# Two chained transformer blocks on one core: four norms computed by halves, the last norm by row tile, a row tile's entry to block two moved into the expert stream, a lent buffer slot returned seven experts later

## The reference, cut to what matters

```python
# first block
h = rmsnorm(x, norm_mix_g);  proj = h @ w_in      # cb cc cx q k v gc ga
merged = sigmoid(gc) * y_conv + sigmoid(ga) * y_attn
x = x + merged @ w_mix_out                        # site "mx"
m = rmsnorm(mem, norm_mem_g)                      # norm ("mem", 1)
x = x + cross_attention(rmsnorm(x, norm_cross_g), m, w_cq, w_ckv, w_co)   # site "co"
hf = rmsnorm(x, norm_ffn_g)                       # norm ("ffn", h)
# peer_ffn: per token 8 heads x 16 experts of 16384, each a row of peer_u and one of peer_v
act = gelu(einsum('td,thkd->thk', hf, peer_u[experts]))
x = x + einsum('thk,thkd->td', g * act, peer_v[experts])
x = rmsnorm(x, final_g)                           # the entry to block two, tag "fa"
# second block
z = rms_norm(x, mix_norm_g) @ w_in                # norm ("mix2", h)
x = x + y @ w_out                                 # site "ou"
x = x + memory_cross_attention(x, mem, ...)       # norm ("x", 2, h), site "xo"
x = x + conv_ffn(x, ...)                          # norm ("ffn2", h), "up", "down"
return rms_norm(x, final_norm_g)                  # tag "fb"
```

## Time and profile before

| | us |
|---|---|
| median of 3 runs | 2889.5 |
| lowest and highest | 2885.08, 2890.11 |
| the profiled execution, its own time | 2889.16 |
| its span, first to last instruction | 2887.4 |
| PE busy | 2419.1 (84%) |
| DVE busy | 1731.8 (60%) |
| ACT busy | 1131.4 (39%) |
| POOL busy | 665.6 (23%) |
| mean of the 16 DMA engines | 290 GB/s |

### The profile page before, as it was taken

The page is one execution under the profiler, slowest core; times in us unless marked ns, Lnnn a source line. Parts: engine busy times, 40 slices in busy tenths (PEclk is TensorE's granted clock), DMA queues, the critical chain, the costliest instruction groups (busy, mean ns, idle before and its releaser), DMA issues.

```text
span 2887.4 us, 31469 instructions
## 1 busy us (share of the span) xinstructions
PE 2419.1 (84%) x11066; PEld 1663.3 (58%) x11066; DVE 1731.8 (60%) x4201; ACT 1131.4 (39%) x2791; POOL 665.6 (23%) x569
## 2 busy tenths in 40 slices
PE   8999999869978658888958678677985799988998
PEld 7786666657744327536626434353864466655873
DVE  2101311498797788676999888787999426312430
ACT  2101301242533765354442578555555224412210
POOL 0000000122344343332233344444323101000110
PEclk9999999989989879999979578888997799999999
DMA  6555343589999999999899999999999653433443
GB/s 206 172 151 165 102 140 130 203 337 372 402 411 416 414 391 390 419 400 397 307 352 396 366 369 420 413 419 418 417 418 417 226 168 106 147 124 95 153 153 116
DMA packets 160973, 838.77 MB, mean 290 GB/s; under 512 B 17400, under 2 KB 21896, under 8 KB 95024
## 3 DMA queue, kind: packets, MB, share of 16 engines
q0 software_dynamic: 73728, 536.90, 45.8%
q1 hardware_dynamic: 82464, 287.75, 28.8%
q10 hardware_dynamic: 4624, 12.11, 1.1%
HBM read 828.27 MB, written 8.41 MB: 290 GB/s over the span
## 4 chain that ended last, share of the span: by engine, by line
PE 52%; DVE 19%; DMA 12%; ACT 12%; issue 4%; POOL 1%; ACTq 0%; DVEq 0%; SPq 0%
PE ps L914 24%; DMA BIG<-in_uv,BIG 11%; DVE BIG L1956 6%; PE ps L1158 5%; PE ps L934 5%; PE ps L935 5%; DVE X L1933 4%; PE ps L915 3%; PE ps L1185 2%; ACT L1451 2%; DVE BIG L1864 1%; DVE BIG L1861 1%; POOL BIG L2173 1%; PE ps L1128 1%; PE ps L1107 1%
## 5 line engine op out<-in xcount | busy, mean ns | idle before, releaser
L2173 POOL DMA_INDIRECT BIG<-in_uv,BIG x512 | 622.5, 1216 | 1617.5 <-DVE BIG L1910 562.3
L914 PE MATMUL ps<-BIG,RING 128*128 128x256 f32 x3472 | 814.1, 387 | 15.0 <-DMA RING<-in_w_cq 4.8
L914 PEld LDWEIGHTS ps<-BIG,RING 128*128 128x128 f32 x3472 | 667.9, 194 | 149.5 <-issue 26.4
L1956 DVE CUSTOM_DVE_ANT_0 BIG<-BIG 128x1024 f32<-128x1024 f32 x512 | 619.0, 1218 | 98.8 <-DMA BIG<-in_uv,BIG 95.9
L1933 DVE SCALAR_TENSOR_TENSOR X<-BIG,small,X 128x1024 f32<-128x1024 f32 x304 | 389.6, 1282 | 74.9 <-ACT small L1455 74.8
L1451 ACT ACTIVATE small<-small 128x1 f32<-128x1 f32 x512 | 102.3, 200 | 607.4 <-DVE small L1956 602.7
L914 PE MATMUL ps<-WK,RING 128*128 128x256 f32 x1232 | 292.7, 391 | 22.4 <-DVE BIG L1712 20.6
L914 PEld LDWEIGHTS ps<-WK,RING 128*128 128x128 f32 x1232 | 239.6, 196 | 63.1 <-DVE BIG L1712 27.2
L934 PE MATMUL ps<-RING,BIG 128*128 128x512 f32 (+1 forms) x448 | 225.1, 584 | 5.6 <-DVE BIG L1691 2.4
L935 PE MATMUL ps<-RING,BIG 128*128 128x512 f32 (+1 forms) x448 | 223.5, 580 | 0.0
L1284 ACT ACTIVATE BIG<-ps 128x256 f32<-128x256 f32 (+2 forms) x143 | 56.5, 396 | 381.6 <-PE ps L915 325.5
(11 more groups left out here) (258 smaller groups left out, 2867.9 us busy)
## 6 DMA issues: line engine op xcount, KB each, us to landing
RING<-in_w_up SPq DMA_DIRECT2D x88, 512.0 KB
RING<-in_w_down SPq DMA_DIRECT2D x66, 512.0 KB
RING<-in_w_pq SPq DMA_DIRECT2D x32, 512.0 KB
RING<-in_w_cc SPq DMA_DIRECT2D x16, 512.0 KB
RING<-in_w_cx SPq DMA_DIRECT2D x16, 512.0 KB
RING<-in_w_cb SPq DMA_DIRECT2D x16, 512.0 KB
RING<-in_w_cv SPq DMA_DIRECT2D x16, 512.0 KB
RING<-in_w_gc SPq DMA_DIRECT2D x16, 512.0 KB
```

Source lines behind the costliest of these rows:

```text
L914: e.matmul(ps[:, 0:256], W[:, j, :], src[:, j, 0:256], start=j == 0, stop=False)
L1956: e.tensor_tensor_reduce(out=u, in0=HF[:, t % 2, :], in1=u, scale=1.0, scalar=0.0, op0=ALU.mult, op1=ALU.add, accum_out=dots[:, k % 8:k % ...
L2173: e.indirect_dma_start(out=slot[i], out_offset=None, in_=I["uv"], in_offset=bass.IndirectOffsetOnAxis(ap=IDX[:, t, c:c + 1], axis=0)).then ...
```

## The change

Six things are changed.

1. **The memory's norm.** In `mixer_0` its squares, root and scaling stay in place, its eight transpose pairs now follow the projection cb.
2. **Four norms by halves**, those in `QUICK`: ("x", 1, 0) behind site mx, ("ffn", 0) behind co, ("x", 2, 1) behind ou, ("ffn2", 1) behind xo. The residual of columns 0 to 511 is ready one group of four chunks earlier than that of columns 512 to 1023. ACT squares the first half then (`quick_first`), runs a square root that only brings in its table, and DVE prepares the mean. After the second half: squares 512 wide, root with the first half's mean as its bias, reciprocal, and scaling in two pieces of 512 columns. A transpose waits for its own half only.
3. **Slot 7** is taken back seven experts after `gates` (3, 3) has been chosen (`back_at`), so expert 300 and not 293 is the first in it.
4. **The entry to block two by row tile** (`enter`). For row tile 2 it now stands at the end of `work`, while the experts of row tile 3 run: gain row, squares, a root that brings in the table, mean, root, scaling, for "fa" and then "mix2". `second(1)` does this for row tile 3 only. The gain row has an address of its own, in the work area and not in half 1's area.
5. **`last(0)`** stands behind the transposes of ("x", 2, 1), its gain row is loaded behind ou, and its store on SP's queue behind the chunks of site xo.
6. **The last down projection.** Chunks 0 to 15 feed all four q as before. Chunks 16 to 21 are held in the six ring slots together, then used for q 0 and 1, for q 2 and for q 3. Behind q 0 and 1 comes the output norm of row tile 2 (`tail_sq`, `tail_out`, `tail_store`), behind q 3 that of row tile 3, both in halves of 512 columns, with the table brought in ahead, and four stores of 128x512. The tuple that `late_down` yields is only written otherwise.

```diff
+QUICK = {("x", 1, 0): "mx", ("ffn", 0): "co", ("x", 2, 1): "ou", ("ffn2", 1): "xo"}
...
-        if i >= (8 if self.lent_from is None or (3, 3) in self.chosen else 7):
+        if self.back_at is None and (3, 3) in self.chosen:
+            self.back_at = k + 7
+        if i >= (8 if self.lent_from is None or (self.back_at is not None and k >= self.back_at) else 7):
...
     def norm_steps(self, key, lean):
+        if key in QUICK:
+            for kind in ("quick_sq", "quick_inv", "quick_out"):
+                yield 0, kind, key
+            return
...
-        yield from self.norm(("mem", 1), False)
+        yield from self.norm_steps(("mem", 1), False)
         yield from self.proj_T("cb", 0, 2, False)
+        for k in range(8):
+            yield 0, "trans", ("mem", 1), k, False
...
         yield from self.norm(("x", layer, h), lean)
+        if layer == 2 and h:
+            yield from self.last(0)
...
+        if h:
+            yield from self.enter(1, 0)
...
         if h:
-            yield from self.last(0)
+            yield 0, "final_in", "fb", 0
         yield from self.cross(2, h, lean)
+        if h:
+            yield 0, "store", 0
...
-            for f in range(22):
+            for f in range(16):
...
+            ring = {f: self.next_ring() for f in range(16, 22)}
+            for f in ring:
+                yield 0, "chunk", "down", f, ring[f]
+            for qs in ((0, 1), (2,), (3,)):
+                for f in ring:
+                    yield 0, "down", h, f, ring[f], qs
+                if qs[-1] % 2:
+                    for kind in ("tail_sq", "tail_out", "tail_store"):
+                        yield 0, kind, qs[-1] // 2
...
         yield from self.second(0, True)
         self.light = True
+        while "total2" not in self.reached:
+            yield "wait"
+        yield 0, "final_in", "fa", 1
+        yield from self.enter(0, 4.0)
...
+            def quick_sq(key):
+                site, src = QUICK[key], norm_of(key)["src"]
+                for i in range(2):
+                    w.wait_ge(*at["ev", site, key[-1], 1, i])
+                    own()
+                    e.activation(SQ[:, 512:1024], src[:, i, 512:1024], ACT.Square, accum_out=small[:, 502 + i:503 + i]).then_inc(
+                        act.sem, act("sqb", key, i))
+                    own()
+                    w.wait_ge(*at["nb", key])
+                    e.activation(small[:, 506 + i:507 + i], small[:, 502 + i:503 + i], ACT.Sqrt, bias=small[:, 504 + i:505 + i],
+                                 scale=1.0 / 1024).then_inc(act.sem, act("rt", key, i))
```

More of the change, by code:

```diff
@@ L1145, in conv_out, with down @@
                     pe.sem, pe("mm", "ct", h, c))
-            def down(h, f, k, tiles):
+            def down(h, f, k, qs):
                 W = RING[:, k % 6, :]
@@ L1150, in down @@
                 w.wait_ge(*at["upm", h, f])
-                qs = [2 * t + hh for t in tiles for hh in range(2)]
                 for q in qs:
@@ new lines, in enter_root, with enter_out @@
+            def enter_root(kind, i):
+                v = small[:, ENTER_AT[kind] + i:ENTER_AT[kind] + i + 1]
+                w.wait_ge(*at["erec", kind, i])
+                e.activation(v, v, ACT.Sqrt).then_inc(act.sem, act("ert", kind, i))
+            def enter_out(kind, i):
+                if kind == "mix2" and i == 0:
+                    own()
+                    w.wait_ge(*at["ev", "up", 0, 10, 3])
+                    e.activation(TMPz[:, 0, :], X[:, 2, :], ACT.Copy, scale=small[:, ENTER_AT[kind]:ENTER_AT[kind] + 1]).then_inc(
+                        act.sem, act("nrm", ("mix2", 1), 0))
@@ L1619, in norm_out, with quick_first, quick_inv @@
                     dve.sem, dve("nrm", key, 1))
+            def quick_first(key):
+                w.wait_ge(*at["sqa", key, 1])
+                e.tensor_scalar(small[:, 504:506], small[:, 500:502], 1.0 / 1024, 1e-6, ALU.mult, ALU.add).then_inc(
+                    dve.sem, dve("nb", key))
+            def quick_inv(key):
+                o = norm_of(key)["o"]
+                for i in range(2):
+                    w.wait_ge(*at["rt", key, i])
+                    e.reciprocal(small[:, o + i:o + i + 1], small[:, 506 + i:507 + i]).then_inc(dve.sem, dve("ri", key, i))
+                at["rstd", key] = (dve.sem, dve.n)
@@ new lines, in quick_out, with enter_inv @@
+            def quick_out(key):
+                n = norm_of(key)
+                own()
+                for j in range(2):
+                    e.tensor_scalar(n["tmp"][:, 1, 512 * j:512 * j + 512], n["src"][:, 1, 512 * j:512 * j + 512],
+                                    small[:, n["o"] + 1:n["o"] + 2], None, ALU.mult).then_inc(dve.sem, dve("nrm", key, 1, j))
+            def enter_inv(kind, i):
+                v = small[:, ENTER_AT[kind] + i:ENTER_AT[kind] + i + 1]
+                w.wait_ge(*at["esq", kind, i])
+                w.wait_ge(*at["ahead", kind, i])
+                e.tensor_scalar(v, v, 1.0 / 1024, 1e-6, ALU.mult, ALU.add).then_inc(dve.sem, dve("emean", kind, i))
+                own()
+                e.reciprocal(v, v).then_inc(dve.sem, dve("erec", kind, i))
@@ new lines, in tail_out @@
+            def tail_out(i):
+                w.wait_ge(*at["tsq", i, 0])
+                e.tensor_scalar(small[:, 518 + i:519 + i], small[:, 508 + 2 * i:509 + 2 * i], 1.0 / 1024, 1e-6, ALU.mult,
+                                ALU.add).then_inc(dve.sem, dve("tb", i))
+                w.wait_ge(*at["trt", i])
+                e.reciprocal(small[:, 520 + i:521 + i], small[:, 520 + i:521 + i]).then_inc(dve.sem, dve("trec", i))
+                own()
+                w.wait_ge(*at["fb", 1])
+                for hh in range(2):
+                    sl = slice(512 * hh, 512 * hh + 512)
+                    e.scalar_tensor_tensor(out=OUT[1][:, i, sl], in0=X[:, 2 + i, sl], scalar=small[:, 520 + i:521 + i],
+                                           in1=FG1["fb"][1][:, sl], op0=ALU.mult, op1=ALU.mult).then_inc(
+                        dve.sem, dve("fin", 1, i, hh))
@@ L2102, in y_scale, with down @@
                         e.tensor_scalar(Y[h][:, i, a:b], Y[h][:, i, a:b], small[:, o:o + 1], None, ALU.mult).then_inc(dve.sem, dve(*sig))
-            def down(h, f, k, tiles):
+            def down(h, f, k, qs):
                 if f == 21:
-                    for q in range(2 * tiles[0], 2 * tiles[-1] + 2):
+                    for q in qs:
                         w.wait_ge(*at["mm", "dn", h, f, q])
```

120 lines of the change are left out of this document (97 added, 23 removed).

## The result

| | before | changed |
|---|---|---|
| median | 2889.81 us (4 runs) | 2859.02 us (4 runs) |
| lowest and highest | 2885.08, 2891.35 | 2857.47, 2860.78 |
| the profiled execution | 2889.16 | 2857.47 |
| its span | 2887.4 | 2855.7 |

The ratio is 0.9896, with a 95% interval of 0.9879 to 0.9914: 31 us (1.0%) faster. The forecast was 2854, with a range of 2846 to 2870. Run again beside the first three experiments the changed kernel had a median of 2857.66.

What follows compares the result with a forecast made beforehand. PE was taken to bound the first and last stages, gathers by DMA the expert stream between. Terms summed to 37.4 us, less 2.4 for the clock 35.0, so 2889.2 became 2854, range 2846 to 2870.

Steps and rivals of the forecast that it cites:

- memory's norm: Between cx and cb: PE's 6.22 us wait goes and the slow transposes and chunk speed up, 8.8 us gained.
- norm ("x", 1, 0): Behind mx: PE already comes to the transposes without a wait, so halves gain 0 and cost nothing.
- norm ffn, with its clock: Behind co: wait of 5.92 us falls to 2.6 (3.3 saved), clock kept up gives 4.3; together 7.6.
- norm ("x", 2, 1), wait: Behind ou: wait of 8.07 us falls to 2.65, with half 0's output norm moved behind the transposes; 5.4 gained.
- its clock: PE's full clock in the transposes and chunk behind the shortened wait: 3.7 us behind ou; 1.4, transposes only, behind xo.
- norm ffn2, wait: Behind xo: PE's wait of 5.92 us falls to 2.6, 3.3 us gained.
- clock risk over all three: Behind co, ou and xo: one in four of the 9.4 us of clock gains charged as lost, -2.4.
- slot 7: Expert stream near 1600 us: POOL's 16.44 us wait at expert 293 goes; 5 us gained, between 0 and 7.2.
- entry in the stream: Row tile 2's entry beside the last experts: gains 0 and costs 1.5 us, between bounds of 0 and -7.5.
- the end: After down's last matmul: chain of 6.4 us instead of 10.8, 0.7 added for chunk 21 and hand-overs; 3.7 gained.
- rival A: PE's clock halves after all three shortened waits, costing 9.4 us instead of 2.4: 2861; chance 0.17.
- C: Table switches hold ACT for twice 1.28 us in the entry, so 5 us lost, not 1.5: 2859; chance 0.08.

Runs made afterwards that it cites:

- the first three experiments: The runs e2, e3 and e4, timed on the same chip as e1, the changed kernel run again unaltered at 2857.66 us.
- e2: Changed kernel with only the memory's transposes put back between cx and cb: 2866.10 us, ratio 0.9922 to the kernel before.
- e1: Changed kernel run again unaltered, as the measure for other runs: 2857.66 us beside 2888.07, ratio 0.9896 to the kernel before.
- e5: Changed kernel with the four norms in one piece again, half 0's output norm still behind the transposes: 2870.76 us, ratio 0.9943.
- e3: Changed kernel with slot 7 given back at the first expert after gates (3, 3), as before: 2864.52 us, ratio 0.9915.
- e4: Changed kernel with row tile 2's entry moved out of the stream, in front of row tile 3's in second(1): 2856.30 us, ratio 0.9882.
- e7: Changed kernel without the two roots that only bring in the table in row tile 2's entry (four table loads less): 2856.15 us, ratio 0.9889.
- e11: As e4, but the 512 KB gain row is still loaded in the stream as in the changed kernel: 2857.50 us, ratio 0.9887.
- e6: Changed kernel with the last down projection's 22 chunks in old order and one output norm for both row tiles: 2863.14 us, ratio 0.9910.
- e8: As e4, with slot 7 given back 14 experts after gates (3, 3) instead of seven: 2856.93 us, ratio 0.9893.
- e12: e4 with the fills of e9 and e10 together: 2856.31 us, ratio 0.9887.
- e10: Changed kernel with throwaway matmuls, 36 before the very first norm's transposes and 12 before projection ya: 2856.37 us, ratio 0.9890.
- e9: Changed kernel with 18 throwaway matmuls in PE's wait before the transposes behind co, ou and xo: 2857.13 us, ratio 0.9892.

## Why the prediction was right, point by point

| term | forecast | measured | from |
|---|---|---|---|
| memory's norm | 8.8 | 8.4 | e2 against e1; 6.22 + 1.69 + 1.10 = 9.0 by the rows at 102.26 and 74.63 |
| norm ("x", 1, 0) | 0 | 0 | no wait before or after |
| norm ffn, with its clock | 7.6 | 7.5 | 3.25 + 1.75 + 2.48, rows at 510.92; e5's first dot 7.3 later |
| norm ("x", 2, 1), wait | 5.4 | 5.4 | rows at 2532.58 |
| its clock | 3.7 | 1.8 | mean of the 10 traces without a fill there |
| norm ffn2, wait | 3.3 | 3.25 | rows at 2619.39 |
| its clock | 1.4 | -0.3 | mean of the same 10 |
| clock risk over all three | -2.4 | in the two lines above | |
| slot 7 | 5 | 5.0 by expert 312, about 3 by the end | traces, e3 |
| entry in the stream | -1.5 | -1.4 | e4, e7, e11 |
| the end | 3.7 | 4.9 | 10.8 to 5.9; e6 5.5 |
| sum | 35.0 | 32.5, with 3 for the slot | |

The total came out nearer than its parts: the slot gave about 2 us less than forecast and the clock 1.3 less, the end 1.2 more. That these partly cancel is luck.

The steps that held: each wait of PE at a norm became the 2.6 to 2.7 us that were worked out from the pieces; the chunk behind the memory's norm regained its clock; the waits of POOL went; and the sum passed through the stream as it was.

**The clock term was mis-sized, with its reason.** I charged one in four, from nine idles of twelve in the expert stream that kept the clock. But I had looked at the first microsecond behind each only. In four of the nine the clock fell 1.4 to 1.7 us after the wait's end, while PE worked on without a pause. One of them is the very example of the earlier trace rows, here two microseconds later in the kernel before:

```profile
1037.00:1038.00 1.00, 1.00 (x8) 0.00 (x0) 1.00 (x3) 0.98 (x3) 0.00 (x0) 0.50 0.99 410
```

The others are the waits that ended at 1007.59, 2103.57 and 2144.45. So seven of the twelve lost the clock and five kept it; charged like that, the term would have been -5.5 and not -2.4 (an estimate, 7/12 of 9.4), and the forecast 2857. At the norms themselves it was again otherwise: behind ou and xo 18 of 20 lost it, and behind co it was kept each time. The measured clock is 5.7 us for the three places (4.2 behind co, 1.8 and -0.3) and not 7.0. For ou and xo together the forecast was 3.8, rival A's figure 0, the measured one 1.5: the rival was nearer there, and wrong behind co.

**The slot's step was right and its end was not.** 5 us were taken from DVE's own waits, and 5.0 came. The prediction took it as final; 0.4 to 3.2 us of it were given back before expert 496, 3 in the changed kernel. That exactly 5.0 came is partly luck, as it was a choice between 0 and 7.2.

**The entry's size was right, its reason half.** The prediction had 1.25 for the row, took -1.5 between the bounds of 0 and -7.5 without saying what the rest was, and gave ACT's 14.7 us a rival of their own (C). e7 and e11 show that ACT's work cost nothing and the row was all. The case that a table switch holds ACT for longer fell as well: the square root at 2218.68 stands 0.01 behind the end of the load at 2217.39 (1.28 us). By the Trainium skill ("ScalarE: Activation LUTs", What ACT_TABLE_LOAD costs) a drain of about 1380 ns would have been added to each of the eight switches; neither trace shows it.

**The end gave 1.2 more**: 5.9 us and not 7.1. The working had 6.4 for the chain, with 3.1 for the store as before; but the stores are half as large now and took 2.0 from issue to landing instead of 2.7. The 0.7 added for the last chunk and the hand-overs wasn't needed either: PE ran the last 176 matmuls of the trace, from 2774.13 on, without a wait. The working for it had counted ten matmuls of 0.43 us as 4.3; each that is written stands as two in the rows, so it is 8.6 us in which chunk 21 can land.

**What the sum had no term for.** The terms as measured make 32.5, the medians differ by 30.8. The 1.7 between is little more than the 1.4 by which one kernel's median moved. Beside the terms the traces show three things that come and go. At the start the clock rose later: the kernel before ran its first chunk in 3.29 us (at 16.84), the changed one in 4.86 (at 17.70), and the chunk after it began 2.4 us later; so it is in e3 and e11, and in none of the others. Before ya 1.7 us were lost in nine of the kernels, not in e2, where the memory's norm stands as before, and not in e8, where it doesn't. And from the down matmuls to y's transposes the kernel before took 228.2 us, the changed one and seven others 224.1 to 224.7, e7, e8 and e12 226.8, e4 and e6 228.2 and 228.0. With a single trace of before, these 3.6 us can't be put down to the change. The first two are PE's clock, at the same instructions, in one execution and not in another; in the third the down matmuls at 2401.47 took 5.57 us before instead of 3.70, at a granted clock of 0.50 from 2401.5 to 2405. That is why single traces with all of the change in front of the stream reach the first dot anywhere from 10.8 to 16.4 us before the old kernel, with a mean of 13.3 for eight of them, where the terms say 15.9 to 16.3. Of the 2.6 to 3.0 us between, 1.5 are ya's loss in seven of the eight, and 0.9 is that the second chunk began that much later in their mean. Why the clock falls before ya in most of the new kernels and not in the old one stays open.

## What to carry to other kernels

A wait of the bounding engine has two prices, its length and the clock behind it. Here the length could be worked out to 0.1 us from the pieces of the old chain, while the clock term was 1.3 us off, since the sample was from another stage and watched for one microsecond: take such samples from the same kind of place, and follow each for as long as the work behind the wait lasts.

At the head of an in-order queue of transfers one wait for something unrelated stops all that would be free behind it; to move the borrower seven places back cost nothing that the traces show, and gave 5 us at once and 3 to 4 by the stream's end. In a saturated DMA stream an added transfer costs what its bytes take, and work on an engine with slack nothing: ask where the bytes go before the instructions.

And a start won in front of a stream that is bound by transfers can be kept, the stream only moves: it was with the memory's norm (e2) and ffn's (e5). With the fills of e10 and e12 3.7 us of it were lost, so it has to be looked at each time.

## What the runs showed of the hardware that was not expected

The same wait of 2.68 us on PE kept the full clock behind co in ten kernels of ten and lost it behind ou or xo in 18 of 20. Throwaway matmuls in the wait kept it in all six of the waits where they were tried (e9, e12). What differs between the places was not found.

A matmul of a 128x128 float32 tile against another ran as two on PE: 18 written, 36 in the trace, 4.18 us, while a transpose of the same size is one of 0.11 us from start to start. The kernel's own matmuls do the same: a chunk's seven at L964 are 14 in its row.

Fills before the first norm and before ya (e10, e12) brought the first dot forward and then 3.7 us of it were lost before expert 292 in both. This stays open.
